# Norms around the feed-forward through a scaled diagonal, and attention's weight splits and K and V copies in another order

## The reference, cut to what matters

```python
def rms_norm(x, g):
    y = x * lax.rsqrt(jnp.mean(x * x, axis=-1, keepdims=True) + RMS_EPS)
    return y * g
h = modulate(rms_norm(x, norm_g[i, 2]), sh2, sc2)     # h * (1 + scale) + shift
h = dense_swiglu(h, ffn_w_in[j], ffn_w_out[j])
x = x + g2[:, None, :] * rms_norm(h, norm_g[i, 3])
...
proj = h @ w_in
cq  = rms_norm(proj[..., :384], q_norm)
ckv = rms_norm(proj[..., 384:640], kv_norm)
q  = (cq @ w_uq).reshape(bsz, seq, 16, 96)
kv = (ckv @ w_ukv).reshape(bsz, seq, 16, 128)          # 64 of K, 64 of V
k  = concat([kv[..., :64], broadcast(rope(k_rope_in))])
s  = causal(q @ k^T * scale);  o = softmax(s) @ v;  return o @ w_o
```

## Time and profile before

| | |
|---|---|
| three runs | 1118.63, 1116.31, 1118.13 us; median 1118.13 |
| the profiled execution | 1116.84 us, of which 1114.9 are the span from its first to its last instruction |
| TensorE busy | 1012.3 us, 91% of the span |
| VectorE busy | 824.8 us, 74% |
| ScalarE busy | 621.1 us, 56% |
| mean granted TensorE clock | 0.957 of 2.4 GHz |

### The profile page before, as it was taken

The page is one execution under the profiler, slowest core; times in us unless marked ns, Lnnn a source line. Parts: engine busy times, 40 slices in busy tenths (PEclk is TensorE's granted clock), DMA queues, the critical chain, the costliest instruction groups (busy, mean ns, idle before and its releaser), DMA issues.

```text
span 1114.9 us, 17888 instructions
## 1 busy us (share of the span) xinstructions
PE 1012.3 (91%) x6770; PEld 837.6 (75%) x6771; DVE 824.8 (74%) x1116; ACT 621.1 (56%) x764; POOL 29.7 (3%) x73
## 2 busy tenths in 40 slices
PE   0776699999999999878989999999999999999993
PEld 0454388888989888656888888888888888888882
DVE  7899885544353647577468898888989898898884
ACT  4420264533333445366347777767677776867762
POOL 3000000000000000000100000000000000000000
PEclk9977789999999999979979999999999999999998
DMA  9848994767868837240347999999999999999951
GB/s 264 312 186 221 264 317 175 249 224 242 301 239 306 319 134 308 91 137 4 131 152 259 363 335 352 317 353 324 343 345 332 351 317 352 320 349 339 330 203 58
DMA packets 199110, 292.98 MB, mean 263 GB/s; under 512 B 18294, under 2 KB 164971, under 8 KB 198779
## 3 DMA queue, kind: packets, MB, share of 16 engines
q1 hardware_dynamic: 189114, 283.32, 73.8%
q10 hardware_dynamic: 8160, 5.85, 1.9%
q0 software_dynamic: 1760, 2.78, 1.1%
HBM read 287.39 MB, written 2.11 MB: 260 GB/s over the span
## 4 chain that ended last, share of the span: by engine, by line
issue 53%; PE 31%; DVE 10%; ACT 3%; DMA 2%; SPq 1%; POOL 0%; ACTq 0%; DVEq 0%; POOLq 0%
PE ps L589 8%; PE ps L590 8%; PE ps L591 8%; PE ps L633 2%; DMA raw<-in_w_ada 1%; SPq L409 1%; PE ps L959 1%; PE ps L950 1%; PE ps L942 1%; PE ps L933 1%; PE ps L744 1%; DVE w_lo L1538 1%; PE ps L755 1%; DVE act_f L1696 1%; PE ps L735 0%
## 5 line engine op out<-in xcount | busy, mean ns | idle before, releaser
L2051 DVE TENSOR_TENSOR w_lo<-raw,w_hi 128x2048 fp32r<-128x2048 f32 x162 | 366.0, 2287 | 64.8 <-ACT w_hi L1455 64.8
L1455 ACT ACTIVATE w_hi<-raw 128x2048 fp32r<-128x2048 f32 x162 | 303.9, 1909 | 0.0
L1538 DVE TENSOR_TENSOR w_lo<-raw,w_hi 128x2048 fp32r<-128x2048 f32 (+3 forms) x59 | 131.7, 2251 | 95.8 <-ACT w_hi L1174 94.4
L589 PE MATMUL ps<-w_hi,xe_hi 128*128 128x512 f32 x448 | 179.3, 400 | 1.4 <-DVE xe_lo L2028 1.4
L591 PE MATMUL ps<-w_hi,xe_lo 128*128 128x512 f32 x448 | 175.4, 392 | 0.0
L590 PE MATMUL ps<-w_lo,xe_hi 128*128 128x512 f32 x448 | 174.8, 390 | 0.0
L1174 ACT ACTIVATE w_hi<-raw 128x2048 fp32r<-128x2048 f32 (+3 forms) x59 | 109.2, 1878 | 73.8 <-DMA raw<-in_ffn_w_in 68.1
L589 PE MATMUL ps<-act_hi,w_hi 128*128 128x256 f32 x352 | 102.1, 290 | 1.5 <-DVE act_lo L1706 1.4
L590 PE MATMUL ps<-act_lo,w_hi 128*128 128x256 f32 x352 | 100.1, 284 | 0.0
L591 PE MATMUL ps<-act_hi,w_lo 128*128 128x256 f32 x352 | 100.1, 284 | 0.0
L589 PEld LDWEIGHTS ps<-w_hi,xe_hi 128*128 128x128 f32 x448 | 84.1, 188 | 17.7 <-DVE w_lo L1538 1.4
(11 more groups left out here) (394 smaller groups left out, 1608.9 us busy)
## 6 DMA issues: line engine op xcount, KB each, us to landing
raw<-in_moe_w_in SPq DMA_DIRECT2D x224, 512.0 KB, 5.1
raw<-in_moe_w_out SPq DMA_DIRECT2D x56, 1024.0 KB, 7.1
raw<-in_w_ada SPq DMA_DIRECT2D x48, 1024.0 KB, 10.2
raw<-in_ffn_w_in SPq DMA_DIRECT2D x44, 512.0 KB, 7.6
raw<-in_ffn_w_out SPq DMA_DIRECT2D x11, 1024.0 KB, 10.3
raw<-in_ssm_w_glu SPq DMA_DIRECT2D x16, 512.0 KB, 8.4
raw<-in_mla_w_o SPq DMA_DIRECT2D x4, 1024.0 KB, 7.7
raw<-in_mla_w_uq SPq DMA_DIRECT2D x3, 768.0 KB, 7.9
```

Source lines behind the costliest of these rows:

```text
L589: mm(dst, st[0], mv[0], start=first, stop=False)
L1455: af(HI[:, (V_MOE + m) % RING, :], RAW[:, (RAW_OF_W[V_MOE] + m) % RING, :], cp).then_inc(hi_done, 1)
L1538: tt_(LO[:, slot, 0:w], RAW[:, RAW_OF_W[v] % RING, 0:w], HI[:, slot, 0:w].bitcast(F32), ALU.subtract)\
L2051: tt_(LO[:, slot, :], RAW[:, (RAW_OF_W[V_MOE] + m) % RING, :], HI[:, slot, :].bitcast(F32), ALU.subtract)\
```

## The change

It has two parts.

**Norms 1 and 2.** VectorE no longer scales the tile of X. It scales the 128 x 128 identity matrix by the reciprocal of each token (`norm_scale`), and TensorE multiplies each piece of X by this diagonal, which transposes and scales it at once (`norm_scaled`). Of the eight column tiles VectorE applies scale and shift to 0, 1, 4 and 5, and ScalarE to 2, 3, 6 and 7. The high halves of 2 to 7 and their low halves are made two column tiles at a time. `keep_warm` has 10 products in place of 14.

**Attention.** Both engines split units 8, 9 and 10 before they come to the copies and rotation of Q, and unit 11 after these, ahead of the copies of K and V; none is left behind these copies. ScalarE computes one exponential of a constant before it waits for the last `w_ukv` product. Its eight copies have another order: K of bank 6, then K and V of banks 0 and 1, and the other three inside the loop of the heads, behind the first head's copy of transposes. TensorE begins `w_ukv` on banks 6 and 7 without a wait and waits for two copies of Q only ahead of bank 0; it waits for copies of K and V in steps, from the first head's transposes to the third's.

The diff without the lines that only name semaphores:

```diff
@@ -667,6 +667,16 @@
                                   src[:, tt, dt * P:(dt + 1) * P], IDENT[:, :])
+                        if tt == TT - 1 and dt % 2:
+                            last.then_inc(n_ps, 1)
+
+            def norm_scaled(m, bank):
+
+                for tt in range(TT):
+                    pe.wait_ge(n_tok, TT * m + tt + 1)
+                    for dt in range(DT):
+                        last = mm(PS[:, bank + dt // 2, (dt % 2) * SEQ + tt * P:(dt % 2) * SEQ + (tt + 1) * P],
+                                  X[:, tt, dt * P:(dt + 1) * P], TOK[:, tt, 0:P], start=True, stop=True)
                         if tt == TT - 1 and dt % 2:
@@ -820,10 +830,10 @@
-            keep_warm(14, 7)
+            keep_warm(10, 7)
             for n in range(24, 28):
                 ada(n)
-            norm(1, TOK, 0)
+            norm_scaled(1, 0)
@@ -872,8 +882,8 @@
             pe.wait_ge(wide_ok, NSEC)
-            keep_warm(14, 7)
-            norm(2, TOK, 4)
+            keep_warm(10, 7)
+            norm_scaled(2, 4)
             pe.wait_ge(res_ok, 2 * TT)
@@ -913,19 +923,25 @@
                 for tt in range(TT):
-                    if k == 0:
-                        pe.wait_ge(q_sb, (2, 6)[tt])
+                    if k == 0 and tt:
+                        pe.wait_ge(q_sb, 6)
                     for b in range(4):
+                        if k == 0 and tt == 0 and b == 2:
+                            pe.wait_ge(q_sb, 2)
                         last = mm3(PS[:, (6 + 4 * tt + b) % 8, :], [x[:, 3 + k, tt * P:(tt + 1) * P] for x in (CQH, CQL)],
...
             pe.wait_ge(q_rope, TT)
-            pe.wait_ge(kf_ok, 8)
-            pe.wait_ge(vv_ok, 8)
             def head_transpose(h):
+                if h < 2:
+                    pe.wait_ge(kv0_ok, 3 + 2 * h)
+                    pe.wait_ge(kv1_ok, 1)
+                if h == 2:
+                    pe.wait_ge(kv0_ok, 8)
+                    pe.wait_ge(kv1_ok, 8)
                 if h >= 2:
@@ -936,6 +952,8 @@
                 pe.wait_ge(qk_sb, h + 1)
+                if h < 2:
+                    pe.wait_ge(kv1_ok, 2 + 2 * h)
                 if h >= 2:
@@ -1234,9 +1252,28 @@
-                for dt in range(DT):
+                s = 6 * (m // 2) + 3 * (m % 2)
+
+                def scaled(dt):
+
+                    act.wait_ge(n_ps, 4 * m + dt // 2 + 1)
+                    return af(H32[:, dt, :], PS[:, (0, 0, 4)[m] + dt // 2, (dt % 2) * SEQ:(dt % 2 + 1) * SEQ],
+                              ACT.Identity, bias=MOD[:, s, dt:dt + 1], scale=MOD[:, s + 1, dt:dt + 1])
+
+                act.wait_ge(mod_ok, 2 * (m + 1))
+                scaled(2)
+                for dt in range(2):
                     act.wait_ge(n_f32, DT * m + dt + 1)
                     af(AH[:, dt, :], H32[:, dt, :], cp).then_inc(n_hi, 1)
+                for n in range(2):
+                    if n:
+                        scaled(6)
+                    scaled(4 * n + 3).then_inc(n_fa, 1)
+                    if n:
+                        act.wait_ge(n_f32, DT * m + DT)
+                        af(AH[:, 4:6, :], H32[:, 4:6, :], cp).then_inc(n_hi, 2)
+                    act.wait_ge(n_fa, 2 * m - 1 + n)
+                    af(AH[:, 4 * n + 2:4 * n + 4, :], H32[:, 4 * n + 2:4 * n + 4, :], cp).then_inc(n_hi, 2)
@@ -1368,7 +1405,7 @@
                 af(CQH[:, i, :], C32[:, i, :], cp).then_inc(p_hi, 1)
-            split_to(V_MLA + 8)
+            split_to(V_MLA + 11)
             act.wait_ge(unit_used, V_MLA + 6)
@@ -1377,14 +1414,24 @@
                         .then_inc(q_sb, 1)
-            split_to(V_MLA + 9)
+            split_to(V_MLA + 12)
+            af(ST[:, 23:24], EPSC[:, :], ACT.Exp)
             act.wait_ge(unit_used, V_MLA + 8)
-            for b in range(4):
+
+            def kv_copy(b, value):
+
                 kv = PS[:, (6 + b) % 8, :].rearrange("p (h d) -> p h d", h=4)
-                af(KF[:, 0, 4 * b:4 * b + 4, 0:NOPE], kv[:, :, 0:NOPE], cp).then_inc(kf_ok, 1)
-                af(VV[:, 0, 4 * b:4 * b + 4, :], kv[:, :, NOPE:], cp).then_inc(vv_ok, 1)
-            split_to(V_MLA + 12)
+                if value:
+                    af(VV[:, 0, 4 * b:4 * b + 4, :], kv[:, :, NOPE:], cp).then_inc(kv0_ok, 1)
+                else:
+                    af(KF[:, 0, 4 * b:4 * b + 4, 0:NOPE], kv[:, :, 0:NOPE], cp).then_inc(kv0_ok, 1)
+
+            for b, value in ((0, 0), (2, 0), (2, 1), (3, 0), (3, 1)):
+                kv_copy(b, value)
             for i in range(H + 5):
+                if i == 1:
+                    for b, value in ((1, 0), (0, 1), (1, 1)):
+                        kv_copy(b, value)
                 if i < H:
@@ -1688,22 +1735,36 @@
+            def norm_scale(m):
+                for tt in range(TT):
+                    dve.wait_ge(n_rt, TT * m + tt + 1)
+                    link_(v_.reciprocal(ST[:, 8 + tt:9 + tt], ST[:, 6 + tt:7 + tt]))
+                    ts_(TOK[:, tt, 0:P], IDENT[:, :], ST[:, 8 + tt:9 + tt], None, ALU.mult).then_inc(n_tok, 1)
+
+            def norm_column(m, dt):
+                dve.wait_ge(n_ps, 4 * m + dt // 2 + 1)
+                a, b = columns(m, dt)
+                return ts_(H32[:, dt, :], PS[:, (0, 0, 4, 0)[m] + dt // 2, (dt % 2) * SEQ:(dt % 2 + 1) * SEQ], a, b,
+                           ALU.mult, ALU.add)
+
+            def norm_lo(m, dt, n=1):
+                dve.wait_ge(n_hi, DT * (m - 1) + dt + n)
+                tt_(AL[:, dt:dt + n, :], H32[:, dt:dt + n, :], AH[:, dt:dt + n, :].bitcast(F32), ALU.subtract).then_inc(n_lo, n)
+
             def norm_columns(m, split=True):
                 dve.wait_ge(mod_ok, 2 * (m + 1))
-                for dt in range(DT):
-                    dve.wait_ge(n_ps, 4 * m + dt // 2 + 1)
-                    a, b = columns(m, dt)
-                    ts_(H32[:, dt, :], PS[:, (0, 0, 4, 0)[m] + dt // 2, (dt % 2) * SEQ:(dt % 2 + 1) * SEQ], a, b, ALU.mult, ALU.add)\
-                        .then_inc(n_f32, 1)
-                    if split and dt >= 2:
-                        norm_lo(m, dt - 2)
-                if split:
-                    norm_lo(m, DT - 2)
-                    norm_lo(m, DT - 1)
-
-            def norm_lo(m, dt):
-                dve.wait_ge(n_hi, DT * (m - 1) + dt + 1)
-                tt_(AL[:, dt, :], H32[:, dt, :], AH[:, dt, :].bitcast(F32), ALU.subtract).then_inc(n_lo, 1)
+                if not split:
+                    for dt in range(DT):
+                        norm_column(m, dt).then_inc(n_f32, 1)
+                    return
+                for dt in range(2):
+                    norm_column(m, dt).then_inc(n_f32, 1)
+                for dt in range(2):
+                    norm_lo(m, dt)
+                norm_column(m, 4).then_inc(n_f32, 1)
+                norm_column(m, 5).then_inc(n_f32, 5)
+                for dt in range(2, DT, 2):
+                    norm_lo(m, dt, 2)
@@ -1849,7 +1910,7 @@
             residual(0, [TOK[:, tt, :] for tt in range(TT)], [(glu_ok, 7), (glu_ok, 8)])
-            norm_rows(1, X, TOK)
+            norm_scale(1)
             norm_columns(1)
@@ -1871,7 +1932,7 @@
             residual(1, banked, [(r_ss, TT + 1), (r_ss, TT + 2)])
-            norm_rows(2, X, TOK)
+            norm_scale(2)
             norm_columns(2)
@@ -1919,20 +1980,19 @@
             dve.wait_ge(k_rope, 4)
-            split_to(V_MLA + 8)
+            split_to(V_MLA + 11)
             for tt in range(TT):
...
                 rotate(qr, qr, tt, H).then_inc(q_rope, 1)
-            split_to(V_MLA + 9)
+            split_to(V_MLA + 12)
             dve.wait_ge(unit_used, V_MLA + 8)
...
                 kv = PS[:, 2 + b, :].rearrange("p (h d) -> p h d", h=4)
-                v_.tensor_copy(KF[:, 1, 4 * b:4 * b + 4, 0:NOPE], kv[:, :, 0:NOPE]).then_inc(kf_ok, 1)
-                v_.tensor_copy(VV[:, 1, 4 * b:4 * b + 4, :], kv[:, :, NOPE:]).then_inc(vv_ok, 1)
-            split_to(V_MLA + 12)
+                v_.tensor_copy(KF[:, 1, 4 * b:4 * b + 4, 0:NOPE], kv[:, :, 0:NOPE]).then_inc(kv1_ok, 1)
+                v_.tensor_copy(VV[:, 1, 4 * b:4 * b + 4, :], kv[:, :, NOPE:]).then_inc(kv1_ok, 1)
             dve.wait_ge(mask_ok, 1)
...
             for i in range(H + 5):
```

More of the change, by code:

```diff
@@ L281, in program @@
         m_in = [sem(f"m_in{i}") for i in range(2)]
-        n_ss, n_rt, n_tok, n_ps, n_f32, n_hi, n_lo = sems("n_ss n_rt n_tok n_ps n_f32 n_hi n_lo")
+        n_ss, n_rt, n_tok, n_ps, n_f32, n_fa, n_hi, n_lo = sems("n_ss n_rt n_tok n_ps n_f32 n_fa n_hi n_lo")
         u_ps, u_ok, v_ps, s_ok, y_ps, yr_ok, yt_ok, zh_ok, zl_ok = sems(
@@ L289, in program @@
             "x_out p_sb p_rt p_nrm p_ps p_f32 p_hi p_lo")
-        cs_arg, cs_ok, q_sb, q_rope, k_rope, kf_ok, vv_ok = sems(
-            "cs_arg cs_ok q_sb q_rope k_rope kf_ok vv_ok")
+        cs_arg, cs_ok, q_sb, q_rope, k_rope, kv0_ok, kv1_ok = sems(
+            "cs_arg cs_ok q_sb q_rope k_rope kv0_ok kv1_ok")
         qk_ps, qk_sb, s_mm, s_max, e_ok, pn_ok, pt_ps, pt_sb, o_mm, o_hi, o_lo = sems(
```

## The result

The changed kernel takes 1106.35 us in the median (1103.44 to 1108.42, four runs), the kernel before 1117.82; the ratio is 0.9894, with a 95% interval of 0.9875 to 0.9914. That is 11.5 us less, and 10.9 in a second set of runs (1105.49 and 1116.39; 0.9902, 0.9882 to 0.9921). The prediction, 1107.9 in a range of 1105.0 to 1111.0, with 10.25 us less, held.

A forecast was written before the change was run, and what follows sets the result against it. TensorE was busy for 91% of the span, so gains had to come from its standstills or its clock. The terms -0.85 - 9.7 + 0.3 = -10.25 us took the median 1118.13 to 1107.9 us, range 1105.0 to 1111.0.

The forecast's parts named there:

- Units 8 to 10 ahead of Q: Before the copies of Q: the moved splits fit where ScalarE and VectorE were idle, at a cost of nothing.
- `w_ukv` starts without Q's copies: Start of `w_ukv`: six products run before Q's copies are awaited, second token tile earlier; 0.85 us gained, bounds 0.5 and 1.27.
- From the last product to the steady heads: First K and V copy to head 1's probabilities: splits and table load leave the chain, at full clock; 9.7 us gained.
- the 26% of the rival: Rival, 26%: TensorE's clock falls at the first heads; up to 2.5 us come back, 1110.4 us.
- The table: Ahead of the first exponential: the table load leaves the chain, 1.28 us gained; the skill's page would make it 1.38 larger.
- The norms: Norms 1 and 2 together: 0.3 us lost, from 0.8 gained to 3.8 lost.
- the end counts: Norm 1: first products wait for every column tile, so the last low half's earlier end decides; 0.3 us gained.
- since then TensorE has a whole input unit in hand ... 0.6 lost: Norm 2: only the first three column tiles count; the third product group waits to about 423.9, 0.6 us lost.
- No change: Rival, 3%: the start of attention is hidden under the experts' weights; 1118 us.
- slower: Rival, 2%: the head loop settles at 1.2 GHz, 4.05 us a head instead of 2.36; 1135 us with all sixteen.
- a split holds Q's copies: Rival, 4%: a split of 1.9 us stands between the last `w_uq` product and Q; 1109.8 us.
- the rival of the dearer norms: Rival, 8%: the norms cost 3.5 us more, with norm 1's clock at 1.2 GHz before; 1111.4 us.

The follow-up runs named there:

- combined kernel: Changed kernel with scaled tiles, plain transposes and shared column tiles in the norms, sines later, warm-up products recounted, 12 fillers ahead of `w_uq`: 1102.96 us, ratio 0.9882.
- norms alone: Kernel before with only the change's part for norms 1 and 2, all of attention as before: 1116.18 us, ratio 1.0000.
- kernel with filler: Kernel before plus 18 unread identity products on TensorE between the second head's transposes and the first scores: 1117.01 us, ratio 0.9986.
- the filler there: Changed kernel plus 12 unread identity products between the projections' transposes and the first `w_uq` product: 1105.49 us, ratio 0.9903.

## Why the prediction was right

**Units 8 to 10 ahead of Q: nothing.** Right; ScalarE had 2.10 us to spare and VectorE 0.66 (1.38 in the second profile, whose `w_uq` products were slower). VectorE is the nearer limit: in the combined kernel 0.15 us are left.

**`w_ukv` starts without Q's copies: 0.85.** 0.83 in the profile, 0.84 when undone.

**From the last product to the steady heads: 9.7.** 9.85, in the parts as forecast: to the copy of transposes at 1.8 (1.84), from there 4.67 (4.46), 2.36 (2.37). Most of the 0.21 us in the middle is a reading: the chain begins the copy of before at 482.95, when the split ahead of it is over, while the timeline has its start at 482.78. The choice of the full clock carried 2.5 us of this and came out right in all eight profiles of this code. It was closer than the 26% of the rival suggest: with one table load (1.4 us) or one late set of copies (2.1 us) more in this stretch the clock fell. And the 18.52 us taken for before depend on the execution; in the profile with the norms alone the same code took 16.85. So the change is worth 8.2 to 9.85 us here, by how long the clock of the kernel before stays down.

**The table.** 1.28 us were forecast against the 2.66 of the Trainium skill, "ScalarE: Activation LUTs", "What ACT_TABLE_LOAD costs". The run without the exponential ahead paid 1.41. Here the measurement decides: no drain of another 1.38 us shows.

**The norms: 0.3 lost.** 0.33 gained; this term was mis-sized, below what a time here can tell. At norm 1 the end of the stage came 0.37 earlier (forecast 0.3); 0.22 of that hang on the clock, which had fallen in norm 1 before, while the same norm without the fall, in the kernel with filler, took 222.86. (With the old norm the clock fell there in two profiles of three, with the new ones in none of eleven.) The last low half was 0.58 earlier and not 0.3, in part because two of ScalarE's column tiles overlap, 1.00 us for both, which I had kept at 0.574 each. But only 0.15 of this arrived at the same clock, so "the end counts" was wrong. TensorE's last wait for a low half, in the kernel with filler and in the changed one:

```profile
206.94 0.39 PE L589 MATMUL ps<-act_hi,w_hi 128*128 128x256 f32 x1 [0.17 <-DVE act_lo L1708]
```

```profile
205.16 0.39 PE L589 MATMUL ps<-act_hi,w_hi 128*128 128x256 f32 x1 [0.43 <-DVE act_lo L1752]
```

Counted from the last gated product these are 14.69 and 14.19 us. The first is for the sixth column tile, the second for the fifth and sixth, with three products more (0.36 us) still to do: 0.14 us gained. Behind these waits the last two tiles are ready in time either way.

The first column tile was 0.19 late (forecast 0.26). At norm 2 the third product group was late as forecast: from the last modulation row's copy it started after 9.28 us and not 8.82. But the 0.6 us that I carried to the end did not arrive. The hand-over from the input projection to ScalarE, before and then after:

```profile
437.07 6.86 PE L661 MATMUL ps<-ident 128*128 128x128 f32 x60
...
437.43 0.23 ACT L1355 ACTIVATE rope_cs<-rope_ang 128x32 f32<-128x32 f32 x1 [5.08 <-DVE rope_ang L1562]
...
437.68 0.47 ACT L1359 ACTIVATE mla_proj<-ps 128x384 f32<-128x384 f32 x1
```

```profile
436.08 0.23 ACT L1392 ACTIVATE rope_cs<-rope_ang 128x32 f32<-128x32 f32 x1 [5.39 <-DVE rope_ang L1609]
...
436.75 6.86 PE L661 MATMUL ps<-ident 128*128 128x128 f32 x60
436.95 0.49 ACT L1396 ACTIVATE mla_proj<-ps 128x384 f32<-128x384 f32 x1 [0.52 <-PE ps L591]
```

Before, TensorE was out of its products at 437.07, and ScalarE came with its copy only at 437.68: it was held by the sine, and this by VectorE's angles. That was 0.4 us of slack, and VectorE's shorter norm had moved the angles forward. The step that failed is "since then TensorE has a whole input unit in hand ... 0.6 lost": true of TensorE, but in the kernel before TensorE was not what the next step waited for.

**What the sum did not have.** The `w_uq` products took 12.60 us for 14.18 in the first profile, 1.6 us of its 13.4. The second profile of the same kernel has 14.21. This is the execution's, not the change's, and a balance of the two first profiles alone would have booked it wrongly. Without it the stages add up to 0.83 + 9.85 + 0.33 = 11.0 us less, beside 11.5 and 10.9 in the two sets of runs. The forecast of 10.25 was 0.75 short, 0.6 of it in the norms.

**The spread.** The forecast's own spread, 1105.3 to 1108.9, does not follow from its terms at the upper end: 1107.9 + 0.5 + 0.8 is 1109.2. The range did not rest on it.

**The rivals.** "No change" and "slower" are refuted by the ratio. That a split holds Q's copies is refuted by the 2.10 us. That the clock falls at the first heads did not happen in either profile of this kernel. The rival of the dearer norms (3.5 us) is refuted by the stages, 0.33 us shorter.

The Trainium skill, "ScalarE: Activation LUTs", "Rules for kernel authors", would keep additions and multiplications on VectorE. The reason it gives is a speed in bf16; in this float32 norm, which waits for a chain through both engines, sharing them with ScalarE (and making halves in pairs) saved 0.5 us at norm 1, at the same clock, and 0.36 at norm 2.

Left open: how often the clock falls ahead of the `w_uq` products, since each kernel has one or two profiles, and so what the filler there is worth in the median.

## What to carry to other kernels

Look behind the last copy of a stage for work that nobody waits for yet, and move it to where its engine stands idle; then ask what the shorter wait does to TensorE's clock, which here was up to 2.7 of the 9.85 us. Products that only keep TensorE busy are cut to a wait: when the wait shrinks they become it, so count them again after every change. Compare stages between marks and not whole profiles, and take a second profile of the same kernel before a difference is explained.

## What the runs showed of the hardware

With the same products and the same stand of 3.16 us ahead of them, the `w_uq` products ran their first microseconds at 1.2 GHz in eleven of twelve profiles and at 2.4 GHz throughout in one: 12.60 to 15.40 us for the same 54 products. With the same stand of 2.92 us between the last `w_ukv` product and the first transposes, the clock fell in that stand or with the first transpose in two profiles, in the longer stand behind the transposes in one, and not at all in one, where filler products stood behind them. Between profiles of different kernels the untouched start (189.8 to 193.9 us) and end (620.4 to 623.4 us) differ by 4 and 3 us; single runs of one kernel lay up to 7.9 us apart (1109.06 to 1116.96), and which stages that comes from is not shown, since each kernel has one or two profiles. A float32 column tile on ScalarE with scale and shift by column takes 0.56 us alone and 0.44 more for the next (1.00 for two), close to VectorE's 0.53 and 0.46 (0.99 for two).
